# The inverse norms of the first layer spread inside the modulation block, its last weight block in two halves, and the odd k-tiles on GpSimd

## What is computed

```
mod = silu(c) @ ada_w + ada_b                      # 9 rows of conditioning: prompt and 8 samples; 6 x 1024 columns
sh1, sc1, g1, sh2, sc2, g2 = split(mod, 6)
h = rmsnorm(x, norms[0]) * (1 + sc1) + sh1         # x * rsqrt(mean(x*x) + eps) * norm
aq, ak, av, af, bq, bk, bv, bg, ca, cb = split_cols(h @ w_in)
```

## Time and profile before

| | |
|---|---|
| median of 3 runs | 2892.43 us (2884.91 to 2892.48) |
| the profiled execution | 2882.91 us, its span 2880.4 us |
| mean granted clock of TensorE | 0.976 |
| PE busy | 2752.8 us (96%) |
| DVE busy | 1772.8 us (62%) |
| ACT busy | 1190.6 us (41%) |
| POOL busy | 195.0 us (7%) |

### The profile page before, as it was taken

How to read it: one execution, slowest core, us unless ns; L and a number is a source line. 1 busy time by engine, 2 the same in 40 slices (tenths; PEclk the granted TensorE clock), 3 DMA queues, 4 the chain that set the end, 5 groups by cost and what they waited for, 6 DMA issues and landing times. The chain is left out here.

```text
span 2880.4 us, 46373 instructions
## 1 busy us (share of the span) xinstructions
PE 2752.8 (96%) x18620; PEld 2440.1 (85%) x18620; DVE 1772.8 (62%) x2865; ACT 1190.6 (41%) x1925; POOL 195.0 (7%) x101
## 2 busy tenths in 40 slices
PE   6999999899999999999949999999999999999998
PEld 4888888788788899999938889887877888999997
DVE  5593445556766765676756743554667667667655
ACT  3241334544444444444422313344444445544444
POOL 1221100110000000000011210102000000000000
PEclk7999999999999999999969999999999999999999
DMA  6842223443333344232228312334333333323322
GB/s 223 250 121 60 68 67 96 118 139 95 93 97 89 94 141 147 81 96 89 70 93 226 90 43 68 88 89 132 129 91 96 95 95 96 89 79 91 95 87 86
DMA packets 439452, 302.02 MB, mean 105 GB/s; under 512 B 28061, under 2 KB 402437, under 8 KB 438438
## 3 DMA queue, kind: packets, MB, share of 16 engines
q1 hardware_dynamic: 433205, 289.39, 34.2%
q10 hardware_dynamic: 6033, 9.67, 1.1%
HBM read 276.07 MB, written 23.78 MB: 104 GB/s over the span
## 5 line engine op out<-in xcount | busy, mean ns | idle before, releaser
L1761 PE MATMUL tslot<-h_hi,w_hi 128*128 128x260 f32 (+1 forms) x2496 | 674.9, 325 | 9.6 <-DVE h_lo L2565 6.2
L1761 PE MATMUL tslot<-h_hi,w_lo 128*128 128x260 f32 (+1 forms) x2496 | 667.0, 322 | 0.0
L1761 PE MATMUL tslot<-h_lo,w_hi 128*128 128x260 f32 (+1 forms) x2496 | 664.9, 321 | 0.0
L1761 PEld LDWEIGHTS tslot<-h_hi,w_hi 128*128 128x128 f32 x2496 | 416.4, 190 | 55.2 <-issue 9.9
L1761 PEld LDWEIGHTS tslot<-h_hi,w_lo 128*128 128x128 f32 x2496 | 415.4, 189 | 37.8
L1761 PEld LDWEIGHTS tslot<-h_lo,w_hi 128*128 128x128 f32 x2496 | 415.6, 190 | 37.2
L1732 ACT ACTIVATE w_hi<-w_raw 128x1024 fp32r<-128x1024 f32 x292 | 307.1, 1052 | 330.0 <-PE tslot L2187 308.4
L1736 DVE TENSOR_TENSOR w_lo<-w_raw,w_hi 128x1024 fp32r<-128x1024 f32 x276 | 336.1, 1218 | 3.1 <-ACT w_hi L1732 3.1
L2650 DVE TENSOR_TENSOR cat<-cat,tslot 128x512 f32<-128x512 f32 (+1 forms) x320 | 220.4, 690 | 185.7 <-PE tslot L2187 185.0
L2187 PE MATMUL tslot<-f_hi,w_hi 128*128 128x260 f32 (+1 forms) x1056 | 283.7, 323 | 6.9 <-DVE w_lo L1736 4.2
L2613 DVE SCALAR_TENSOR_TENSOR bufs<-bufs,vecs 128x512 f32<-128x512 f32 x176 | 132.0, 750 | 252.5 <-ACT bufs L2442 252.3
(11 more groups left out here) (370 smaller groups left out, 3798.7 us busy)
## 6 DMA issues: line engine op xcount, KB each, us to landing
w_raw<-in_ffn_up_dram SPq DMA_DIRECT2D x176, 512.0 KB, 3.9
w_raw<-in_ffn_down_dram SPq DMA_DIRECT2D x88, 512.0 KB, 3.8
x_res<-in_ada_w_dram SPq DMA_DIRECT2D x64, 512.0 KB, 5.3
w_raw<-in_w_in_dram SPq DMA_DIRECT2D x48, 512.0 KB, 4.6
w_raw<-in_w_o_dram SPq DMA_DIRECT2D x32, 512.0 KB, 5.5
x_hold<-x_res SPq DMA_DIRECT2D x2, 4128.0 KB, 17.0
x_res<-x_hold SPq DMA_DIRECT2D x2, 4128.0 KB, 12.7
a_raw<-in_ada_w_dram SPq DMA_DIRECT2D x4, 2048.0 KB, 22.4
```

The source lines that it names most:

```text
L1761: last = pe.matmul(out[:, at + a:at + b], w[:, kk, :], x[:, kk, t0 + a:t0 + b], start=(kk == 0 and first), stop=(kk == KD - 1 and w is w_lo))
```

## The change

Five parts. The fourth early weight load is issued as two loads of 256 columns each, with a semaphore of their own. The modulation block has five pieces (`PIECES`), the last two being the halves of weight block 3. In TensorE's list the token sums stand ahead of product 2, and their result goes into columns 480 to 488 of the bank of the vectors in place of a bank of their own; the order is product 0, product 1, the vectors, turn 0, token sums, product 2, turn 1, first half product, turn 2, the spread, second half product, turn 3, turn 4. Vector writes the diagonal right behind the inverse norms; diagonal and spread are gone from `block_project`, and `slot0` is allocated before the entry block and handed on. `POOL_LOWS` is (1, 3, 5, 7). The rest of the diff is allocation: `slot0` and `k_ret` get scopes of their own, for both layers.

```diff
-            for b in range(4):
+            for b in range(3):
                 sp.dma_start(k.a_raw[b][:, :, :], ada[:, :, BANK * b:BANK * b + BANK]).then_inc(k.a_early[b], 16)
+            for h in range(2):
+                sp.dma_start(k.a_raw[3][:, :, 256 * h:256 * h + 256], ada[:, :, BANK * 3 + 256 * h:BANK * 3 + 256 * h + 256]
+                             ).then_inc(k.a_early[3 + h], 16)
...
+        rb = k.slot0
+        diag = sb("mod_diag", [P, TC, P])
...
-        vp, st = ps("vp", [P, BANK]), ps("mst", [P, BANK])
+        vp = ps("vp", [P, BANK])
+        st = vp[:, 480:480 + TC]
...
+        PIECES = [(b, 0, W) for b in range(BLOCKS - 1)] + [(BLOCKS - 1, 0, W // 2), (BLOCKS - 1, W // 2, W)]
...
-            for b in range(BLOCKS):
-                pe.wait_ge(w_loaded[b % RING], 16 * (b // RING + 1))
-                if b >= 2:
-                    pe.wait_ge(row_ready, b - 1)
+            for n, (b, low, high) in enumerate(PIECES):
+                if b == 2:
+                    pe.wait_ge(summed, KD - 1)
+                    pe.wait_ge(scaled, 4)
+                    pe_token_sums(k, pe, st, acc, True, True).then_inc(sums_ready, 1)
+                pe.wait_ge(w_loaded[n], 16)
+                if n >= 2:
+                    pe.wait_ge(row_ready, n - 1)
                 for kk in range(KD):
...
-                if b == 1:
+                if n == 1:
                     rows_of_vectors()
-                if b >= 1:
-                    turn(b - 1)
-                if b == 2:
-                    pe.wait_ge(summed, KD - 1)
-                    pe_token_sums(k, pe, st, acc, True, True).then_inc(sums_ready, 1)
-            turn(BLOCKS - 1)
+                if n >= 1:
+                    turn(n - 1)
+                if n == BLOCKS - 1:
+                    pe.wait_ge(diag_ready, 1)
+                    pe_spread(k, pe, diag, rb)
+            turn(BLOCKS)
...
-            for b in range(BLOCKS):
+            for n, (b, low, high) in enumerate(PIECES):
                 if b == 2:
                     dve.wait_ge(sums_ready, 1)
                     dve_inverse_rms(k, dve, link, st, v, t)
-                dve.wait_ge(turned, b + 1)
...
+                    dve_diagonal(k, dve, diag).then_inc(diag_ready, 1)
+                dve.wait_ge(turned, n + 1)
...
-POOL_LOWS = (0, 2, 4, 6)
+POOL_LOWS = (1, 3, 5, 7)
...
-            if L == 0:
-                pe.wait_ge(diag_ready, 1)
-                pe_spread(k, pe, diag, slot[0]).then_inc(rb_ready, 1)
...
-                dve_diagonal(k, dve, diag).then_inc(diag_ready, 1)
-                dve.wait_ge(rb_ready, 1)
                 normed.on_dve(dve)
```

## The result

The changed kernel takes 2898.60 us in the median of 20 runs (2887.32 to 2904.58), the kernel before 2890.22 in the median of 20 (2879.80 to 2894.40). The ratio is 1.0026, 95% interval 1.0017 to 1.0036: slower by 5 to 10 us, clear of zero and near the 0.3% named as the limit. Forecast were 2901.0 and +8.6. The two profiled executions have spans of 2880.4 and 2889.5 us, 9.1 apart.

What follows compares the result with a forecast made beforehand. TensorE, busy 96% of the span, was taken as the bound, so early delays pass on whole. Modulation block 7.2 (4.35 Sync's) plus 1.35 behind GpSimd's last start gave +8.6 on the median 2892.43: 2901.0 us, range 2890 to 2906.

Steps and rivals of the forecast that it cites:

- The fifth early load: Entry block's end: the fifth issue waits in Sync's full queue, so all engines start the modulation block late, +4.35 us.
- The modulation block: Sums, product and turn in series before the inverse norms, at 1.2 GHz: samples' rows +7.2 us, 4.35 of it Sync's.
- The other parity: First projection tile, GpSimd on odd k-tiles: the early start is paid back at the last k-tile, 0 within 0.2 us.
- What follows GpSimd's last start: Store of x and conditioning weights behind GpSimd's later last start: +1.35 us, TensorE's wait growing to 2.7.
- Rival (d): First conditioning product: as the sum, but the 2.7 us wait lets the clock fall, +10.3, 2902.7; chance 0.09.
- The walk at full clock: Modulation block walked with all pieces at full clock: samples' rows start at 59.3, +0.7 us.
- (a): Modulation block: start delayed, but clock stays at 2.4 GHz through sums and spread, +2.0, 2894.5; chance 0.12.
- (c): Modulation block on time and clock high, diagonal and spread leave the path behind the barrier: -2.4, 2890.1; chance 0.04.
- (b): Entry block's end: fifth issue short, modulation block starts on time with the clock low, +4.2, 2896.7; chance 0.09.

Runs made afterwards that it cites:

- e1: Kernel before with only its fourth early weight load split by columns into two: 2892.61 us, ratio 1.0011.
- e9: Kernel before with five early loads, the fourth cut by k-tiles 7 to 1 (896 and 128 rows): memset at 31.93 us, one run, no ratio.
- e7: Kernel before with GpSimd on the odd k-tiles and nothing else changed: 2883.12 us, ratio 0.9990.
- e3: Changed kernel with GpSimd on the even k-tiles 0, 2, 4 and 6 again: 2896.12 us, ratio 1.0017.
- e4: Changed kernel with the store of x issued early, at the projection block's start: 2894.73 us, ratio 1.0013.
- e2: Changed kernel with four early loads again, both half pieces waiting for the fourth: 2893.35 us, ratio 1.0011.
- e8: Changed kernel with four loads, block 3 whole, sums behind turn 1, spread as TensorE's last work, early store, even k-tiles on GpSimd: 2887.92 us, ratio 1.0000.
- e12: Changed kernel with four loads, block 3 whole, sums behind turn 1, spread as TensorE's last work, early store, odd k-tiles on GpSimd: 2886.22 us, ratio 0.9992.
- e6: Changed kernel with four early loads and the token sums behind turn 1 again: 2891.67 us, ratio 1.0014.
- e5: Kernel before with five early loads, the fourth cut by k-tiles 4 to 4 (512 rows each): memset at 29.89 us, one run, no ratio.
- e10: Changed kernel with the second half of the last weight block loaded from Scalar's queue, Sync issuing four loads: 2894.50 us, ratio 1.0017.
- e11: Kernel before with odd k-tiles on GpSimd and the store of x at the projection block's start: 2891.52 us, ratio 1.0008.

## Why the prediction was right

The forecast was +8.6 us, measured are +8.4 between medians and +9.1 between the two traces. The mechanism held in its three costs: Sync held at the entry block's end, a longer modulation block, and GpSimd's later last start. The closeness of the number is in part luck. Step by step:

- **The fifth early load** was forecast at +4.35 and cost 5.09 (e1: 4.79). That Sync is the last at the entry block's end and that nothing hides it held. What failed is its reason, "that it fills by rows and not by bytes": e9's 128 rows held Sync as long. The two and a third outstanding loads of the earlier trace rows, given for it, fit a count of loads as well as one of rows. The number came out since the term was taken from the pace of the neighbouring issues, and these were alike whatever their size.
- **The modulation block** was forecast at +7.2 - 4.35 = +2.85 and measured +1.05. The order is the one walked: sums at 44.42 for 43.65, product behind them to 51.37 for 51.3, spread 3.81 for 3.81. Mis-sized were the pieces ahead of the diagonal, which was ready at 56.44 for 57.4 though the block began 0.74 later than forecast. The clock rose at the turn (1.06 for 1.8), which I had at 1.2 GHz throughout. The sums took 3.53 for 4.0 at the low clock: a 1-column matmul costs 0.20 there, and 0.224 was that of a 9-column one. The product gave 0.3, and what stands between turn and diagonal 0.2. And the term as a whole is one pair of traces in a block that moves by 4 us without an edit (e7), so neither +2.85 nor +1.05 is confirmed; that the change's three traces of it (33.06 to 33.91) lie above the three of before (28.35 to 32.76) is all they show.
- **The other parity**: first tile's start 4.73 behind the samples' rows for 4.65, GpSimd's last start 17.64 for 17.6, the tile's end 21.79 for 21.65. "The early start is paid back at the last k-tile" held in the change and in e7: the second tile starts 24.96 and 24.97 us behind the samples' rows, 25.03 before.
- **What follows GpSimd's last start**: +1.21 for +1.35, TensorE's wait 2.57 for 2.7. In the marks e3 and e4 take it away by two different edits.
- **Rival (d)**, the clock falling in that wait, was priced at +1.7 and given 0.09. It came, with 1.54. It is absent where the wait is 1.16 or none (e3, e4) and present in e2, where it is 2.74. So the trace is that of (d), 10.3 by its own sum, and the forecast's sum without it came nearer only because the block was shorter. My argument against it, that a wait of 1.3 us changed nothing, said nothing of 2.6.

So the sum is right with errors that cancel: a shorter block (1.8 less), against a longer hold of Sync (0.7) and the clock behind the wait (1.54). The walk at full clock was also added up wrongly: its own terms give a start at 58.8, not 59.3, so that (a) is +1.5 and (c) -2.9. Of the other rivals, (b) and (c) needed a short fifth issue and fell with the trace; (a) came in part. In (b) I wrote of a rule of the Trainium skill (DMA: Bandwidth & Descriptors, Anatomy of one DMA), by which issuing costs little; the 5.93 and 6.18 us of Sync in these runs disagree with carrying it over to this queue.

What the change was given for its costs is also in the traces: the diagonal and the spread left the stretch behind the barrier, 5.25 us, and came back inside the block as sums, product and turn in series ahead of the inverse norms, and as a spread ahead of the last half product. With four loads (e2) the samples' rows start at 58.94 for 58.63 before: of the gain that was meant nothing is seen.

## What to carry to other kernels

Count every transfer issue at a place where all engines meet: behind large loads one more issue, even of 128 rows, held its queue for 4 to 7 us here, and the whole core with it. Work moved ahead of a barrier can only pay if it runs beside what ends last there; of the spread between two pieces of TensorE's list no gain is seen, and as TensorE's last work (e8, e12) none is shown. A mark in a trace is good for what moves more than it does between traces of the same program: here 2.3 us for the memset with four loads, but 4.4 us for the modulation block of before. A change of a few microseconds needs both, marks from several traces and some twenty runs.

## What the runs showed of the hardware that was not expected

**The clock makes two groups of runs.** From the mixer mark to the end of the span the traces take 2652.9 to 2654.0 us (before 2653.6, change 2653.9, e1 2654.0, e6 2653.5, e7 2652.9, e9 2653.9) or some 8 us more (e2 2661.4, e3 2661.1, e5 2662.6, e8 2661.2, e10 2661.3, e11 2661.6, e12 2661.1; e4 2665.5). The change does not touch this part. The twenty runs of the changed kernel part in the same way: five took 2887.32 to 2891.71 us with a mean granted clock of 0.973 or 0.974, fifteen 2897.72 to 2904.58 with 0.968 to 0.971. Windows of the change and of e3, the same program there, differ in the clock:

```profile
644.00:652.00 8.00, 6.63 (x49) 6.04 (x50) 6.36 (x19) 1.91 (x4) 0.00 (x0) 1.00 0.46 132
...
2000.00:2008.00 8.00, 8.00 (x43) 6.75 (x43) 0.00 (x0) 1.34 (x2) 0.21 (x1) 1.00 1.01 273
```
```profile
642.00:650.00 8.00, 7.33 (x36) 7.33 (x37) 4.86 (x16) 1.21 (x2) 0.00 (x0) 0.57 0.46 134
...
2000.00:2008.00 8.00, 8.00 (x33) 6.95 (x33) 0.07 (x1) 0.00 (x0) 0.00 (x0) 0.57 0.95 265
```

In the first stretch TensorE has pauses in both, and the clock falls in one only. In the second it falls with TensorE busy for all of the 8 us. Such falls make a spread about as large as the effect studied, and nothing in the two programs decides them. The traces of before and of the change are both of the shorter kind, so their difference holds none of it.

**A short Vector instruction can stand behind GpSimd.** In e12 one of the twelve inverse-norm instructions on 9 columns took 2.25 us in place of 0.17, while GpSimd was in its 2.4 us subtraction:

```profile
44.79 2.25 DVE L163 SCALAR_TENSOR_TENSOR inv<-mt,inv 128x9 f32<-128x9 f32 x1
47.07 0.17 DVE L161 TENSOR_TENSOR mt<-inv 128x9 f32<-128x9 f32 x1
```

The Trainium skill (SBUF — State Buffer, Who interferes with whom) says that a VectorE instruction with two SBUF inputs contends with a GpSimd instruction that reads SBUF, and that the one that comes second waits for the whole of the other. This row agrees, as does the 2.43 us low part in the earlier trace rows. In the trace of the kernel before it did not strike the inverse norms; in e7, with the same block, it struck one of them (2.21 us), so it comes and goes without an edit.
